# Scans of a hybrid diffusion step: another order on ScalarE, VectorE and TensorE for a Silu, a skipped input and a transposed result

## The reference, cut to what matters

```python
xbc = silu(dwconv_centred(xbc, conv_w, conv_b))      # inputs xs, and B and C
...
y_f, s_f = ssd_scan(xs, dt[:, :, 0], a[0], bm, cm, init_f)
y_b, s_b = ssd_scan(xs[:, ::-1], dt[:, ::-1, 1], a[1], ..., init_b)
y = y_f + y_b[:, ::-1] + ssd_d[:, None] * xs         # the skipped input
y = y * silu(z)
y = y * rsqrt(mean(y * y) + eps) * ssd_norm_g        # per group of 512 channels
```

## Time and profile before

| what | value |
|---|---|
| median of 3 runs | 3063.99 us (3062.77 to 3068.85) |
| profiled execution | 3068.86 us, span 3066.9 us |
| PE busy | 2335.1 us, 76% of the span |
| DVE busy | 2206.3 us, 72% |
| POOL busy | 1274.6 us, 42% |
| ACT busy | 1266.5 us, 41% |
| mean granted clock of TensorE | 0.864 |
| result_lo, four instructions of one stream | 1.12 us |
| result_hi, four instructions of one stream | 1.12 us |
| stores of one stream's result, two issues | 0.58 and 0.54 us |

### The profile page before, as it was taken

One profiled execution on the slowest core, in us unless ns is written; L12 is line 12 of the kernel. 1 busy time (PEld: TensorE's weight loads), 2 busy tenths in 40 slices (PEclk: granted clock), 3 DMA queues, 4 the chain that ended last, 5 costly groups with the idle time before them and its releaser, 6 DMA issues.

```text
span 3066.9 us, 38874 instructions
## 1 busy us (share of the span) xinstructions
PE 2335.1 (76%) x15054; PEld 2054.5 (67%) x15054; DVE 2206.3 (72%) x2801; ACT 1266.5 (41%) x2063; POOL 1274.6 (42%) x825
## 2 busy tenths in 40 slices
PE   7899999999999899999999950000233329999997
PEld 2588889988888798999997950000132328888886
DVE  1344446877888873444454599999999988989988
ACT  1233334545555563333334320000597924434433
POOL 0000000245555530000000652588788856767763
PEclk8799999999999999999999985555555569999999
DMA  9887776544454459876554367899999978999996
GB/s 377 342 305 292 291 290 216 181 150 158 165 179 139 151 192 358 334 256 238 199 196 165 136 252 289 300 422 422 422 421 421 421 288 294 362 367 376 357 365 237
DMA packets 152794, 868.47 MB, mean 283 GB/s; under 512 B 18865, under 2 KB 31169, under 8 KB 74705
## 3 DMA queue, kind: packets, MB, share of 16 engines
q1 hardware_dynamic: 68578, 449.03, 39.7%
q0 software_dynamic: 73872, 406.08, 34.2%
q10 hardware_dynamic: 10160, 10.88, 1.0%
HBM read 836.81 MB, written 27.39 MB: 282 GB/s over the span
## 4 chain that ended last, share of the span: by engine, by line
PE 46%; DVE 17%; POOL 13%; DMA 11%; issue 9%; ACT 3%; DVEq 0%; SPq 0%; ACTq 0%; POOLq 0%
PE bank L1789 28%; POOL u_ring L734 13%; PE bank L1775 7%; PE bank L2189 4%; DMA v_got<-in_v_rest,expert 4%; DMA raw<-in_tiles 3%; DVE w_lo L1195 3%; PE bank L1814 2%; DMA u_ring<-in_peer_u,expert 2%; DVE u_ring L1649 2%; DVE peer_g L1690 2%; DMA v_raw<-in_v_dense 2%; DVE conv L1309 1%; DVE c_lo L1703 1%; DVE y_w L1367 1%
## 5 line engine op out<-in xcount | busy, mean ns | idle before, releaser
L1195 DVE TENSOR_TENSOR w_lo<-raw,w_hi 128x1024 fp32r<-128x1024 f32 x450 | 600.0, 1347 | 542.3 <-ACT w_hi L779 536.7
L779 ACT ACTIVATE w_hi<-raw 128x1024 fp32r<-128x1024 f32 x482 | 501.1, 1058 | 639.0 <-PE bank L1789 342.1
L1789 PE MATMUL bank<-h_lo,w_hi 128*128 128x256 f32 x2048 | 592.2, 289 | 12.3 <-DVE h_lo L1241 9.0
L1789 PE MATMUL bank<-h_hi,w_lo 128*128 128x256 f32 x2048 | 581.5, 284 | 0.0
L1789 PE MATMUL bank<-h_hi,w_hi 128*128 128x256 f32 x2048 | 581.5, 284 | 0.0
L734 POOL DMA_INDIRECT u_ring<-in_peer_u,expert x256 | 492.6, 1924 | 199.2 <-DVE act_p L1649 120.4
L1649 DVE CUSTOM_DVE_ANT_0 u_ring<-u_ring,h_t 128x2048 f32<-128x2048 f32 x192 | 435.6, 2289 | 21.1 <-DMA u_ring<-in_peer_u,expert 19.4
L741 POOL DMA_INDIRECT v_got<-in_v_rest,expert x256 | 362.0, 1414 | 179.7 <-DVE peer_g L1690 137.3
L1789 PEld LDWEIGHTS bank<-h_lo,w_hi 128*128 128x128 f32 x2048 | 394.6, 193 | 55.3 <-issue 25.3
L1789 PEld LDWEIGHTS bank<-h_hi,w_lo 128*128 128x128 f32 x2048 | 394.9, 193 | 0.9
L1789 PEld LDWEIGHTS bank<-h_hi,w_hi 128*128 128x128 f32 x2048 | 394.5, 193 | 0.0
(11 more groups left out here) (317 smaller groups left out, 4835.7 us busy)
## 6 DMA issues: line engine op xcount, KB each, us to landing
raw<-in_tiles SPq DMA_DIRECT2D x337, 1024.0 KB, 5.5
v_raw<-in_v_dense SPq DMA_DIRECT2D x128, 660.0 KB, 7.3
s_t<-in_states POOLq DMA_DIRECT2D x8, 512.0 KB, 7.3
y_hi_rows<-y_hi_e POOLq DMA_DIRECT2D x16, 256.0 KB, 2.4
y_lo_rows<-y_lo_e POOLq DMA_DIRECT2D x16, 256.0 KB, 6.3
gate_rows<-gate_buf ACTq DMA_DIRECT2D x8, 512.0 KB, 5.3
y_hi<-y_hi_rows POOLq DMA_DIRECT2D x8, 512.0 KB, 8.0
y_lo<-y_lo_rows POOLq DMA_DIRECT2D x8, 512.0 KB, 4.1
```

The costliest lines, as they stand in the source:

```text
L779: act.activation(w_hi[:, i % RING], raw[:, slot % SLOTS, (n % 2) * 2 * CH:(n % 2 + 1) * 2 * CH], ACT.Copy) \
L1195: dve.tensor_tensor(w_lo[:, i % RING], raw[:, n // 2 % SLOTS, (n % 2) * 2 * CH:(n % 2 + 1) * 2 * CH], w_hi[:, i % RING].bitcast(F32), ALU. ...
L1789: ins = pe.matmul(spot if x.shape[1] == KT else spot.rearrange("p (s t) -> p s t", s=NS), w[:, col], moving, start=start and k == 0 and m ...
```

## The change

Three steps of each window stand at other halves. On ACT the Silu of the next inputs stands at t14 and no longer behind norm(g, 1) at t15, and result_hi(g, 0) stands at t15, ahead of norm(g, 1). On DVE skipped(g, 1) stands at t12, behind mix(g, 1), and result_lo(g, 0) at t15. On PE turn_result(g, 0) stands at t14, behind products(g, 1). No instruction is added or taken away by hand, and no wait is changed.

```diff
@@ -910,11 +910,10 @@
                         norm(g, 0)
                     elif t == 11:
                         final_states(g)
-                    elif t == 13:
+                    elif t == 15:
                         result_hi(g, 0)
-                    elif t == 15:
                         norm(g, 1)
-                if t == 15 and w < GROUPS:
+                if t == 14 and w < GROUPS:
                     conv_act(4 + w, conv[:])
 
             def side(n):
@@ -1401,15 +1400,15 @@
                         skipped(g, 0)
                     elif t == 9:
                         combine(g, 0)
-                    elif t == 10:
-                        skipped(g, 1)
                     elif t == 11:
                         mix(g, 1, 0)
                         mix(g, 1, 1)
-                    elif t == 13:
-                        result_lo(g, 0)
+                    elif t == 12:
+                        skipped(g, 1)
                     elif t == 14:
                         combine(g, 1)
+                    elif t == 15:
+                        result_lo(g, 0)
                 if 8 <= t < 12 and w < GROUPS:
                     convolve("xs", w, t - 8)
 
@@ -1979,10 +1978,10 @@
                     products(g, 0)
                 elif t == 9:
                     final_states(g)
-                elif t == 12:
-                    turn_result(g, 0)
                 elif t == 13:
                     products(g, 1)
+                elif t == 14:
+                    turn_result(g, 0)
 
             def spread_g1(j):
```

## The result

| | before | after |
|---|---|---|
| median of 20 runs each, side by side | 3065.16 us | 3075.31 us |
| profiled execution, its own time | 3068.9 us | 3074.66 us |
| its span | 3066.9 us | 3072.8 us |
| granted clock, mean of the span | 0.864 | 0.863 |
| from the first segments to the last transposes of the scans | 528.5 us | 539.4 us |

The ratio is 1.0032, with an interval of 1.0023 to 1.0041: slower by about 10 us, where the forecast was a change too small to tell. 3075.3 lies just above the range's upper end of 3074.5.

A forecast was written before the change was run, and what follows sets the result against it. TensorE's queue plus its gaps was taken as the bound until about 1,760 us; 7 x 0.2 = +1.4 us, less 0.5 for a possible first-window lead, together +1 on 3064.0: 3065 us, range 3055.5 to 3074.5.

The forecast's parts named there:

- What bounds the scans: In the scans VectorE makes TensorE wait; closing three waits totalling 37.7 us would mostly rename them.
- The replay of the window: One scan window worked through instruction by instruction on four engines with the change: +0.2 us a window.
- GpSimd's queue: Stores awaiting the moved lower part delay four masks; half t19's remainder waits for one: TensorE waits 1.4 us, +0.2 a window.
- The bound: At half t19's remainder VectorE loses from 0 to a whole mask: -1.1 to +0.6 us a window.
- the clock term: TensorE half-speed stretches behind new waits at halves 16 and t19: 0 to +12 us, taken as none.
- clock behind the new wait: Rival: TensorE falls to half speed after half t19's wait in five of seven windows, +10 us: 3074; 21%.
- the +1.4 of the sum: Seven scan windows at +0.2 us each; the eighth adds nothing.
- Seven table loads more: On ScalarE z's Silu no longer shares a table load with the inputs' Silu; each load takes 1.28 us.
- The 2% rival: ScalarE's table switch costs what the skill page says, 1.4 us more a window, +9.8 us: 3075; 2%.
- "Right if": Signs of a right forecast: windows of 66.3 to 66.7 us, half t19's remainder over 2 us, seven table loads more.
- the sign that I had named for the clock: Sign of a wrong forecast: scan windows over 67.2 us with more half-clock stretches.
- masks out of the way: Rival: VectorE slips in ahead of GpSimd's masks at half t19, -1.1 us in seven windows, -7.7: 3056; 22%.

The follow-up runs named there:

- e8: Kernel after, with the first stream's transposes (turn_result) at t13 ahead of the products instead of t14: ratio 1.0032 to the kernel before.
- e11: Kernel after, with the second stream's two m_lo masks on GpSimd held until VectorE's remainder of half t20: ratio 0.9971 to the kernel before.
- e14: Kernel after, with the stores of the first stream's result put behind the second stream's four masks in GpSimd's order: ratio 0.9982 to the kernel before.
- e10: Kernel before, with only the inputs' Silu moved to t14 and the second stream's m_lo masks held until the remainder of half t20: ratio 0.9977.
- e3: Kernel before, with only the first stream's transposes moved to t14 and its result_hi and result_lo to t15: ratio 1.0025.
- e4: Kernel before, with the whole change except the skipped input, which stays at t10: ratio 1.0032.
- e15: Kernel after, with the first stream's transposes at t13 ahead of the products and the second stream's m_lo masks held: ratio 0.9969 to the kernel before.

## Why the prediction was wrong, step by step

**What bounds the scans: right in the main.** Closing three waits on TensorE changed their names, and VectorE sets the time where they stand. Between half t19 and half 13 TensorE runs without a wait, and there its own speed counts, as shown below. (The nine tenths of TensorE's line reach to slice 23, not 24; nothing hangs on it.)

**The replay of the window: right to 0.3 us.** Counted from the end of the decay product (812.08 in the replay, 816.47 in the trace after):

| step | replayed | measured |
|---|---|---|
| the pair of the skipped input | 5.3 us | 5.2 (819.45 to 824.63) |
| start of half t16 | +9.5 | +9.6 |
| second gate product done | +12.1 | +11.9 |
| first mask starts | +15.8 | +15.5 |
| remainder of half t19 asked for | +19.9 | +19.8 |
| the same, done | +22.5 | **+24.0** |

The agreement of half t16 is partly luck. I had it waiting 1.5 us for its remainder in every window. It did so in one of seven; in the window of the table it started when half 15 let it, after two stretches of 3.4 us at half speed (from 811.4 and 818.2). The inputs' transposes behind it run without a wait; they were replayed to end at +18.2 and ended at +18.0 (834.49).

**The step that failed: GpSimd's queue.** "VectorE asks for the remainder of half t19 at 832.0, in the middle of the third: it is done at 833.5 + 1.1." The time at which it asks was right, and so was the mask. Wrong was that VectorE gets its turn when the running mask ends. It got it when the fourth had ended too, one mask of 1.9 us later, less what the phase gave back: 1.5 us. TensorE's wait is 2.95 instead of 1.4. Counted on TensorE, half t19 starts 24.0 us behind the products in five windows of seven, where the replay has 22.5 (834.6 less 812.1). That is 5 x 1.5 = 7.5 us. In the other two it starts 22.8 and 22.5 us behind them, as replayed, though VectorE lost one mask or none there.

The bound failed with it. "VectorE may lose from 0 to a whole mask" took the turn-taking of the earlier trace rows as a rule. It holds in nearly every case that the traces have (last section), but not in this one, and the sign of the change hung on it. The upper end should have been two masks, +2.5 us a window instead of +0.6, and with it the range to about 3081.

**The other step: the clock term, taken as nothing.** It measured 3.0 us. "I take none, because TensorE's idle time in a window barely changes": the sum barely changed, but the idle time moved to a place with no wait behind it. From the start of half t19 to the end of the 1.90 us wait for the remainder of half 13, TensorE has no other wait. This stretch takes 39.8 us in two windows and 38.3 or less in the other four that have one (the kernel after; the stretch; busy us and instructions of PE, PEld, DVE, ACT, POOL; granted clock, DMA share, GB/s):

```profile
704.00:743.80 39.80, 37.88 (x233) 33.50 (x233) 34.70 (x38) 15.10 (x22) 19.30 (x10) 0.96 0.43 159
772.40:810.70 38.30, 36.39 (x233) 32.28 (x233) 36.24 (x38) 16.29 (x24) 21.00 (x11) 1.00 0.46 165
```

The same work takes 1.5 us more where 3.4 us at half speed follow the 3 us wait at half t19 (from 705.6, and from 842.1 in the window of the table). This is the rival "clock behind the new wait", in two windows and not in five. Its total (3074) came nearly true, by luck: most of the loss has another mechanism. With the +1.4 of the sum, the masks' 7.5 and these 3.0 make 11.9 us. The first window gives back 1.5 (52.95 us from the first segments to its products, 54.41 before), of which the sum had 0.5. That makes 10.4 of the measured 10.9, as an estimate: it takes the seventh window, where the kernel before has a slow stretch of its own, like the others.

In two other windows half speed saves time. There 6.8 us of it follow a 2.85 us wait at the products (the first row; the second is the window of the table):

```profile
749.65:772.20 22.55, 22.54 (x132) 20.49 (x132) 16.26 (x15) 15.90 (x23) 15.08 (x9) 0.85 0.33 117
...
816.50:837.60 21.10, 21.08 (x132) 18.86 (x132) 14.80 (x15) 14.45 (x21) 14.22 (x9) 0.92 0.36 126
```

TensorE comes to half t19 1.4 us later. The segments come later too, so the masks start 0.6 us later, while VectorE asks at the same time (19.7 us behind the products): it meets the start of the third mask and loses one turn, or comes ahead of it and loses none. These two windows escape the 1.5 us of the five. So by my estimate from these rows the clock costs about 3 us and saves about 3, which fits e8: one stretch behind half t19 instead of two, six collisions instead of five, the same time.

**Smaller steps.** Seven table loads more: right (2063 to 2070). Their price was right too. ScalarE's timeline after, at z's Silu:

```profile
832.91 1.28 ACT L1000 ACT_TABLE_LOAD   x1
834.21 1.09 ACT L1000 ACTIVATE z_g<-bank 128x512 f32<-128x512 f32 x2
```

From the load's start to the Silu's is 1.30 us, all of it the load (1283 ns). The seven new loads are those of z's Silu. The inputs' Silu keeps its seven, and starts 1.3 us behind each load too. The Trainium skill ("ScalarE: Activation LUTs", What ACT_TABLE_LOAD costs) adds a drain of about 1380 ns to it, 2.66 us in all. The trace does not agree here: 834.21 - 832.91 = 1.30. The 2% rival is out.

"Right if" asked for windows of 66.3 to 66.7 us and a remainder over 2 us. The remainder was over 2 us in six windows. The mean of the first six windows is 68.1 us against 66.4, and there is more time at half speed: the sign that I had named for the clock came, and most of it is the masks.

**The rival "masks out of the way" was right as a mechanism.** I gave it 22% and 3056. Made to happen, it is 3055.5 us (e11) and 3058.2 (e14) beside 3063.5 and 3063.3 of the kernel before: 8.1 and 5.1 us below, against 7.7 worked out. The change holds that gain, over half of it perhaps by the Silu alone (e10: 4.4), and GpSimd's queue takes it.

What stays open: why VectorE loses two turns in this phase (below), and how much of e3's and e4's loss the clock carries.

## What to carry to other kernels

When work that moves later feeds a store, look at what stands behind that store in its queue: here two store instructions dragged four masks onto a third engine's critical instruction, and moving the stores (e14) or half of the masks (e11) turned a loss of 0.3% into a gain of 0.2 to 0.3%. Where two engines share SBUF, expect a collision to cost what is left of the other's running operation, but bound it by two of them where more stand back to back. And replay the window to the tenth of a microsecond if the sign hangs on a phase, but give the phases on both sides their full price in the range.

## What was unexpected of the hardware

**Who gets SBUF next.** The same two instructions, a weight remainder on VectorE and the third and fourth mask on GpSimd, asked for in nearly the same phase, end in opposite ways. In the kernel before, VectorE and then GpSimd:

```profile
797.96 2.31 DVE L1195 TENSOR_TENSOR w_lo<-raw,w_hi 128x1024 fp32r<-128x1024 f32 x1
```

```profile
797.29 1.90 POOL L625 TENSOR_TENSOR m_lo<-up_eq,da_lo 128x1024 fp32r<-128x1024 f32 x1
799.14 2.88 POOL L625 TENSOR_TENSOR m_lo<-low_eq,da_lo 128x1024 fp32r<-128x1024 f32 x1
```

VectorE was busy up to 797.96, asked 0.67 us after the mask had begun, and got the turn behind it: 2.31 us, and the next mask waited (2.88). At 836.27 in the kernel after it had been idle for 5.75 us, asked 0.61 us after the mask had begun, and lost to that one and the next: 4.22. The idle time alone does not decide it. In e4 (all but the skipped input) VectorE was idle as long, asked 0.55 us after a mask had begun, and won the next turn (VectorE, then GpSimd):

```profile
829.32 2.43 DVE L1194 TENSOR_TENSOR w_lo<-raw,w_hi 128x1024 fp32r<-128x1024 f32 x1 [5.75 <-ACT w_hi L779]
```

```profile
828.77 1.89 POOL L625 TENSOR_TENSOR m_hi<-low_eq,da_hi 128x1024 fp32r<-128x1024 f32 x1
830.63 2.88 POOL L625 TENSOR_TENSOR m_lo<-up_eq,da_lo 128x1024 fp32r<-128x1024 f32 x1
```

In the scans of the fourteen traces, over 400 remainders are asked for while a GpSimd operation runs and another stands right behind it. All but eleven end 1.1 to 1.2 us behind the running one, whether VectorE was busy before or idle for up to 7.7 us. The eleven are five in the kernel after and six in e8: all asked for 0.59 to 0.61 us into the third mask after 5.75 us of idle time, all 4.2 us long. The phase alone does not decide it either: asked for at 0.62 us with VectorE busy before, the remainder won every time. The Trainium skill ("SBUF — State Buffer", Who interferes with whom) states that whoever issues first gets the shared port pair for the whole instruction, and that issue order decides who blocks. The traces agree for the holder. In the eleven cases they do not agree for the order of the waiting: VectorE's start is recorded 1.25 us ahead of the fourth mask's (836.27 and 837.52), and the mask went first.

**Half speed that costs, costs nothing, or saves.** Between 30.7 and 51.2 us at half speed (e8 and the kernel after) the scans differ by 0.3 us. A stretch of 3.4 us costs 1.5 us where TensorE has no wait behind it, up to the next one that follows VectorE (704.00 to 743.80). It costs nothing where a wait for VectorE behind it shrinks by as much (e11 and e15: 44.4 and 34.1 us at half speed, scans of 522.8 and 522.6). And 6.8 us of it behind the products moved the masks by 0.6 us and spared a collision of 1.5 us.
